# Two transformer blocks on one core: the rotary step's exchange of neighbouring partitions, by a shuffle on VectorE in place of a permutation matmul on TensorE

## What is computed

```python
def apply_rope(x, cos, sin):
    x1 = x[..., 0::2].astype(jnp.float32)
    x2 = x[..., 1::2].astype(jnp.float32)
    y1 = x1 * cos - x2 * sin
    y2 = x1 * sin + x2 * cos
    return jnp.stack([y1, y2], axis=-1).reshape(x.shape).astype(x.dtype)

# first_block, for each layer l:
q, k, v, up, ca, cb = project_inputs(h, w_in[l], q_norm_g[l], k_norm_g[l])   # q, k: rms_norm over 64 features of a head
q = apply_rope(q, cos, sin)
k = apply_rope(k, cos, sin)
k_all = jnp.concatenate([kc, k], axis=3)
attn = diff_attn_post(diff_attention(q, k_all, v_all, lam), subln_g[l], lambda_init)
conv_o = conformer_conv(ca, cb, conv_dw_w[l], ...)      # 31 taps
```

## Time and profile before

| | us |
|---|---|
| median of 3 runs (lowest, highest) | 1655.34 (1654.33, 1656.04) |
| span of the profiled execution | 1652.8 |
| PE busy in it | 1595.9 (97%) |
| DVE busy | 1120.9 (68%) |
| ACT busy | 921.6 (56%) |
| POOL busy | 132.4 (8%) |

### The profile page before, as it was taken

How to read it: one execution, slowest core, us unless ns; L and a number is a source line. 1 busy time by engine, 2 the same in 40 slices (tenths; PEclk the granted TensorE clock), 3 DMA queues, 4 the chain that set the end, 5 groups by cost and what they waited for, 6 DMA issues and landing times. The chain is left out here.

```text
span 1652.8 us, 31090 instructions
## 1 busy us (share of the span) xinstructions
PE 1595.9 (97%) x12890; PEld 1465.8 (89%) x12890; DVE 1120.9 (68%) x1763; ACT 921.6 (56%) x1467; POOL 132.4 (8%) x106
## 2 busy tenths in 40 slices
PE   5999989999999999989999999999999999999999
PEld 2987578999999999966899999878999998799999
DVE  2799667645566655897754556777887567788873
ACT  3444656645365444647554445766666467676662
POOL 0230000112001100300012100000011000001110
PEclk8999999999999999999999999999999999999999
DMA  9433666656546555435466553314555633235553
GB/s 386 161 147 142 255 230 232 228 223 233 194 167 222 200 187 200 154 128 217 172 216 201 187 198 130 117 56 144 194 200 187 216 118 118 78 132 203 206 190 120
DMA packets 45164, 301.09 MB, mean 182 GB/s; under 512 B 5232, under 2 KB 7504, under 8 KB 11744
## 3 DMA queue, kind: packets, MB, share of 16 engines
q1 hardware_dynamic: 44304, 297.44, 50.6%
q0 software_dynamic: 288, 0.92, 0.1%
q10 hardware_dynamic: 432, 0.75, 0.1%
HBM read 298.02 MB, written 1.06 MB: 181 GB/s over the span
## 5 line engine op out<-in xcount | busy, mean ns | idle before, releaser
L2018 DVE TENSOR_TENSOR wl<-raw,wh 128x1040 fp32r<-128x1040 f32 (+1 forms) x472 | 567.3, 1241 | 313.1 <-ACT wh L1771 220.6
L1771 ACT ACTIVATE wh<-raw 128x1040 fp32r<-128x1040 f32 (+1 forms) x472 | 465.5, 1030 | 182.7 <-PE bank L1560 95.2
L1555 PE MATMUL bank<-hx_hi,wh 128*128 128x256 f32 x1856 | 522.6, 282 | 6.0 <-ACT hx_hi L1771 3.8
L1560 PE MATMUL bank<-hx_lo,wh 128*128 128x256 f32 x1856 | 516.7, 278 | 0.0
L1558 PE MATMUL bank<-hx_hi,wl 128*128 128x256 f32 x1856 | 514.6, 277 | 0.2 <-DVE wl L2018 0.2
L1555 PEld LDWEIGHTS bank<-hx_hi,wh 128*128 128x128 f32 x1856 | 349.1, 188 | 12.8 <-issue 11.8
L1558 PEld LDWEIGHTS bank<-hx_hi,wl 128*128 128x128 f32 x1856 | 349.0, 188 | 4.3 <-issue 3.6
L1560 PEld LDWEIGHTS bank<-hx_lo,wh 128*128 128x128 f32 x1856 | 348.9, 188 | 1.2 <-DVE hx_lo L2011 0.4
L1558 PE MATMUL bank<-hid_hi,wl 128*128 128x256 f32 x912 | 252.2, 277 | 1.1 <-DVE wl L2018 1.1
L1555 PE MATMUL bank<-hid_hi,wh 128*128 128x256 f32 x912 | 252.4, 277 | 0.1
L1560 PE MATMUL bank<-hid_lo,wh 128*128 128x256 f32 x912 | 252.0, 276 | 0.0
(11 more groups left out here) (219 smaller groups left out, 1909.1 us busy)
## 6 DMA issues: line engine op xcount, KB each, us to landing
raw<-in_wts SPq DMA_DIRECT2D x208, 1032.0 KB, 4.9
raw<-in_wts SPq DMA_DIRECT2D x50, 1024.0 KB, 6.5
raw<-in_wts SPq DMA_DIRECT2D x20, 776.0 KB, 4.2
raw<-in_wts SPq DMA_DIRECT2D x4, 584.0 KB, 4.2
tmp<-tscr SPq DMA_DIRECT2D x16, 128.0 KB, 3.9
raw<-in_wts SPq DMA_DIRECT2D x2, 648.0 KB, 3.9
xTc<-in_ctxT SPq DMA_DIRECT2D x1, 1024.0 KB, 10.8
xTx<-in_xT SPq DMA_DIRECT2D x1, 1024.0 KB, 8.1
```

Of the source, the lines that this page charges most:

```text
L1555: pe.matmul(out, block(f, M.wh, w0 + k, ncols, c, m), x_hi, start=first and k == 0 and o == 0, stop=False, skip_group_check=True)
L1560: ins = pe.matmul(out, block(f, M.wh, w0 + k, ncols, c, m), x_lo, start=False, stop=last and k == nk - 1, skip_group_check=True)
L1771: return act.activation(out, in_, func, bias=bias, scale=scale)
L2018: tt(M.wl[k][:, cols], M.raw[r][:, cols], M.wh[k][:, cols].bitcast(F32), ALU.subtract).then_inc(*on.inc(lo))
```

## The change

In the rotary step of the first block the neighbour's value no longer comes from PE. DVE copies `xg` into `y` with the partitions of each pair exchanged (`stream_shuffle`, the pattern `PAIRS` applies to every group of 32 partitions), waits for that, and multiplies `y` with the sines in place. The signs that the permutation matrix held now lie in the table of sines. The matrix leaves the constants (`cst` 128x768 becomes 128x640; the memory behind it stays unused, so that all other addresses remain). Bank `r` and the event `t_r` go; DVE waits for ACT's `xg` (`t_xg`) instead.

```diff
+PAIRS = [i ^ 1 for i in range(32)]
...
-    j1 = np.zeros((P, P))
-    for i in range(64):
-        j1[2 * i + 1, 2 * i] = -1
-        j1[2 * i, 2 * i + 1] = 1
-    c["swap1"] = j1
...
-    sn = np.sin(ang.astype(np.float64))[:, dim].T
+    sn = np.sin(ang.astype(np.float64))[:, dim].T * np.where(np.arange(P) % 2, 1, -1)[:, None]
...
-        cst = sb("cst", [P, 6 * P])
+        cst = sb("cst", [P, 5 * P])
+        cur[0] += 4 * P
...
             s, t_s = banks.get(), ev("mm")
-            r, t_r = (None, None) if swap is None else (banks.get(), ev("mm"))
-            s_free, r_free = s.free, r and r.free
+            s_free = s.free
...
-                y, t_d = tmps.get(), [ev("rope") for _ in range(4)]
+                y, t_d = tmps.get(), [ev("rope") for _ in range(5)]
                 y_free = y.free
-                banks.give(r, t_d[0])
...
-            tmps.give(xg, t_d[0] if swap is None else t_d[2])
+            tmps.give(xg, t_d[0] if tables is None else t_d[3])
...
 # tensor_program
-    def hn2(s, s_free, r, r_free, sq, t_sq, xg, t_xg, blk, swap, np_, t_s, t_r, **_):
+    def hn2(s, s_free, sq, t_sq, blk, np_, t_s, **_):
         on.wait_ge(t_sq, s_free)
         mm(s.t[0:np_, :], blk, sq.t[0:np_, :], True, True).then_inc(*on.inc(t_s))
-        if swap is not None:
-            on.wait_ge(t_xg, r_free)
-            mm(r.t[0:np_, :], swap, xg.t[0:np_, :], True, True).then_inc(*on.inc(t_r))
...
 # vector_program, hn2
-        on.wait_ge(t_r, t_tab, y_free)
-        tt(v(y.t), v(r.t), wide(S), ALU.mult).then_inc(*on.inc(t_d[0]))
-        tt(v(xg.t), v(xg.t), wide(C), ALU.mult).then_inc(*on.inc(t_d[1]))
-        on.wait_ge(t_d[1])
-        tt(v(y.t), v(y.t), v(xg.t), ALU.add).then_inc(*on.inc(t_d[2]))
-        on.wait_ge(t_d[2], t_rs, out_free)
-        tt(out, v(y.t), v(rs.t), ALU.mult).then_inc(*on.inc(t_d[3]))
+        on.wait_ge(t_xg, t_tab, y_free)
+        dve.stream_shuffle(y.t[:, :], xg.t[:, :], PAIRS).then_inc(*on.inc(t_d[0]))
+        on.wait_ge(t_d[0])
+        tt(v(y.t), v(y.t), wide(S), ALU.mult).then_inc(*on.inc(t_d[1]))
+        tt(v(xg.t), v(xg.t), wide(C), ALU.mult).then_inc(*on.inc(t_d[2]))
+        on.wait_ge(t_d[2])
+        tt(v(y.t), v(y.t), v(xg.t), ALU.add).then_inc(*on.inc(t_d[3]))
+        on.wait_ge(t_d[3], t_rs, out_free)
+        tt(out, v(y.t), v(rs.t), ALU.mult).then_inc(*on.inc(t_d[4]))
```

More of the change, by code:

```diff
@@ L91, in shape_constants @@
     c["flip"] = np.eye(P)[::-1]
-    sq = np.concatenate([c[k] for k in ("ident", "ones", "bones", "swap1", "swap2", "flip")], axis=1)
+    sq = np.concatenate([c[k] for k in ("ident", "ones", "bones", "swap2", "flip")], axis=1)
     t = np.arange(T)
@@ L219, in __init__ @@
         b1_off = cur[0]
-        self.ident, self.ones, self.bones, self.swap1, self.swap2, self.flip = (
-            cst[:, P * i:P * i + P] for i in range(6))
+        self.ident, self.ones, self.bones, self.swap2, self.flip = (
+            cst[:, P * i:P * i + P] for i in range(5))
         self.V = lambda k: vec[:, VT[k][0]:VT[k][0] + VT[k][1]]
@@ L626, in plan_program, with heads_norm @@
     region_free = []
-    def heads_norm(b, tok, gain, nfeat, blk, swap, tables, out, out_free, np_=P):
+    def heads_norm(b, tok, gain, nfeat, blk, tables, out, out_free, np_=P):
         sq, xg = tmps.get(), tmps.get()
@@ L642, in rest @@
             banks.give(s, t_ln)
-            if swap is None:
+            if tables is None:
                 y, y_free, t_d = None, None, [ev("rope")]
             else:
-                y, t_d = tmps.get(), [ev("rope") for _ in range(4)]
+                y, t_d = tmps.get(), [ev("rope") for _ in range(5)]
                 y_free = y.free
-                banks.give(r, t_d[0])
-            step("hn2", s=s, s_free=s_free, r=r, r_free=r_free, sq=sq, t_sq=t_sq, xg=xg, t_xg=t_xg, rs=rs,
-                 rs_free=rs_free, y=y, y_free=y_free, blk=blk, swap=swap, tables=tables, nfeat=nfeat, np_=np_,
-                 out=out, out_free=out_free, t_s=t_s, t_r=t_r, t_ln=t_ln, t_rs=t_rs, t_d=t_d)
-            tmps.give(xg, t_d[0] if swap is None else t_d[2])
+            step("hn2", s=s, s_free=s_free, sq=sq, t_sq=t_sq, xg=xg, t_xg=t_xg, rs=rs,
+                 rs_free=rs_free, y=y, y_free=y_free, blk=blk, tables=tables, nfeat=nfeat, np_=np_,
+                 out=out, out_free=out_free, t_s=t_s, t_ln=t_ln, t_rs=t_rs, t_d=t_d)
+            tmps.give(xg, t_d[0] if tables is None else t_d[3])
             if y:
@@ L739, in project1 @@
             rest = heads_norm(b, tk, M.V(("qg" if part[0] == "q" else "kg", l)), 64, M.bones,
-                              M.swap1 if s == "x" else None, (M.cosx, M.sinx, t_b1), out, flat(ow))
+                              (M.cosx, M.sinx, t_b1) if s == "x" else None, out, flat(ow))
             def fin():
@@ L1214, in dil_piece @@
                 i = j % 2
-                rest = heads_norm(b, tk, M.V(("gdq" if j < 2 else "gdk", l)), 64, M.bones, None, None,
+                rest = heads_norm(b, tk, M.V(("gdq" if j < 2 else "gdk", l)), 64, M.bones, None,
                                   dst[:, 2 * i:2 * i + 2, :], rf)
@@ L2070, in modend, with hn2 @@
                     ALU.mult).then_inc(*on.inc(t_s[2 + s]))
-    def hn2(r, xg, t_xg, rs, y, y_free, tables, np_, out, out_free, t_r, t_rs, t_d, **_):
+    def hn2(xg, t_xg, rs, y, y_free, tables, np_, out, out_free, t_rs, t_d, **_):
         v = lambda x: x[0:np_, :].rearrange("p (a t) -> p a t", a=2)
-        if r is None:
+        if tables is None:
             on.wait_ge(t_xg, t_rs, out_free)
```

## The result

| | before | after |
|---|---|---|
| median of 5 runs (lowest, highest), us | 1655.27 (1653.64, 1656.04) | 1661.08 (1659.71, 1663.43) |
| span of the profiled execution, us | 1652.8 | 1659.2 |

The ratio is 1.0039, with a 95% interval of 1.0028 to 1.0050. The change makes the kernel slower, by 4.6 to 8.3 us, where I had +2.8 as likeliest and "no difference that can be told" as the likeliest outcome. The time lies inside my range, but the change is twice the one forecast. The profiled execution is 6.4 us longer, and its two traces can be laid side by side, since nearly every instruction has its counterpart.

The account below looks back on a forecast made before the run. DVE's queue, not PE, was taken to pace the changed stretches. First layer 0.57, second layer 2.4 and start -0.15 summed to +2.8 us, 1655.3 to 1658.2 us; range 1653.5 to 1661.5.

Parts of the forecast that it names:

- d = 0.80: DVE time in us added per shuffle at eight places: 0.72 for the shuffle, 0.08 for its pattern; bounds 0.49 and 1.2.
- Rival 1: The shuffle is dear on DVE, d 0.9 to 1.2, giving 1658.9 to 1660.9 us; chance 0.33.
- PE's start at the k1 gemm: First layer, about 138 us: the gemm inherits the matmul's wait and starts some 0.7 us later, not 2.66 us earlier.
- My three signs of being wrong: DVE idle for PE at 140 to 168 us; shuffle far from 0.8 us; PE's 1.31 us wait at 739.63 not growing.
- takes back 0.86 us with the fourth matmul: First layer, 156 us: PE regains 0.86 us, so is about where it was at 172.95, its sum over the taps.
- 4d - 2.63 = 0.57: First layer: four shuffles delay DVE by 3.2 us, less 2.63 us of slack at its end; loss 0.57 us.
- 3d = 2.4: Second layer: three of four shuffles delay the last taps, which PE awaits at 739.63 without slack; loss 2.4 us.
- The third shuffle: Second layer, q1: hidden, since DVE's 0.98 us wait for ACT at 727.61 takes in one d of 0.80.
- The wait at 739.63: Second layer: PE's wait for DVE's last taps was to grow from 1.31 to about 4 us or more.
- Start, -0.15: Load at the start: constants smaller by one 128x128 matrix, 64 KB, save 0.15 us, or zero if the load's end doesn't matter.
- another loss, of a few us: Remaining case: a loss in the tight web of attention units at 170 to 210 us; chance 0.05.

Follow-up runs that it names:

- the four superfluous matmuls: Changed kernel with q1's sum of squares (x, first layer) done five times instead of once, in PE's idle time ahead of the k1 gemm: 1.0017, 1658.51 us.
- the old constants: Changed kernel, all eight shuffles, but constants kept at 128x768: 1.0036 to the kernel before.
- the filler: Same run as the four superfluous matmuls: 512-column matmuls added to the changed kernel at q1 of x, first layer: 1.0017, 1658.51 us.
- the kernel with shuffles and late taps: Changed kernel with eight convolution taps moved from ahead of the first layer's first maxima to behind its first attention weights: 1.0024, 1659.94 us.
- the one with four late taps: Kernel before, permutation matmuls kept, with four taps moved behind the first layer's first attention weights: 0.9993, 1654.51 us.
- the small fillers: Changed kernel with four superfluous matmuls of 128 columns instead of 512, ahead of the first layer's k1 gemm: 1.0030, 1660.63 us.

## Why the prediction was wrong

**The shuffle's price: right.** d = 0.80 was forecast and 0.77 measured (0.74 us long, eight of them between 0.72 and 0.75). The pattern's load is 0.01 to 0.02 us and not 0.08. Rival 1, the dear shuffle, is out, though the outcome it stood for (slower) came. The estimate from the Trainium skill (VectorE: DVE Perf Modes, The perf-mode tier table (the rule you actually need)), 0.80 us long, was 0.06 too high, and the charge of its section The TRN2 errata for PSUM sources is not seen: 0.68 from PSUM, 0.69 from SBUF.

**PE's start at the k1 gemm: about right in time, wrong in what follows.** I forecast it some 0.7 us later than before; in the trace it is 0.2 later, or 1.1 when the start's -0.91 is taken out. I also named the reason, that the wait for the exponentials only passes from the matmul to the gemm. What I did not ask is what 5 us of idle time do to PE. My three signs of being wrong did not catch it: DVE shows no idle time for PE from 140 to 168 us. The step that failed is the sentence that PE "takes back 0.86 us with the fourth matmul (at 156 us), and is about where it was when it reaches the row at 172.95". It would be, at full clock. The gemm took 2.4 us longer, and behind it PE and no longer DVE is late at the end of the layer: in the earlier trace rows the sum over the taps starts at 172.95; after, it starts at 174.76, 2.5 us after the taps are done (170.99 + 1.27).

**First layer, 4d - 2.63 = 0.57: wrong, and in two ways.** With the clock kept up by the four superfluous matmuls, the layer ends 1.06 us later by its own start (the split at 99.71 comes at 98.50, the weights' use at 177.54 at 177.39). So DVE's part was 1.06 us; with the measured d the term gives 0.45. The slack was 2.06 us, DVE's own wait for PE's sum, and not 2.63: I added 0.57 us that stand behind the weights, but the convolution's chain through ACT (175.76, waiting 0.58 us) had no such reserve. The rest of 2.72 us, 1.7 us, is the clock in this pair of traces. It is not a fixed price: with the old constants and with shuffles in the first layer only, the clock falls too, the gemm takes 7.4 and 7.6 us instead of 8.4, and the product with v, at 202.88 us after, comes 1.7 and 1.9 us later than before by its own start, which leaves the clock 0.6 and 0.9 us. In the first of them part of the time at the lower clock passed while PE was idle.

**Second layer, 3d = 2.4: right.** 2.58 in the trace and +2.5 us in the run with the second layer alone. The third shuffle was hidden as forecast: the wait of 0.98 us ahead of q1's last multiplication is 0.19 after. The wait at 739.63 did grow, but only from 1.31 to 1.49 us, and not to 4: the gemm ahead of it ran at a clock of 0.50 (730 to 735 us, behind 4.08 us of idle time) and filled the gap. In six other traces with one shuffle at each place of this layer, as here, the wait was 1.64 us once and shrank five times, to 0.18 to 0.53 us, though the shuffles were there. So that row misleads as a test: it was one of my three signs of being wrong. The multiplication beside GpSimd's last work was slowed to 1.25 us in q0's step, in place of the add in the earlier trace rows.

**Start, -0.15: not seen**, and not to be seen, since the start differs by more than that from one execution to another.

**Not in the sum at all:** the clock of the first layer (1.7 us in the trace), the half microsecond in the output projection, where the clock is at 0.50 in both kernels but for longer after, and the late weights at 784 us (1.2 us). Of my cases the remaining one, with a chance of 0.05 for "another loss, of a few us", comes nearest, but I had placed it at 170 to 210 us and had no clock in mind. With the filler, whose trace has neither the first nor the last of these, the kernel measures +2.8 us (1.3 to 4.1), which is the sum that I had forecast. That it agrees to the tenth is luck, as the first layer's term was 0.6 us too small.

## What to carry to other kernels

When an edit takes work off an engine that then waits for another, write down how long its new idle time is, and look at the granted clock behind the idle times that the profile already has. At this gemm 1.5 to 1.8 us of it left the clock alone, and 3.6 us and more did not; elsewhere in the same traces two shorter waits close together were enough. Work taken off TensorE beside a queue of VectorE can then be worth nothing (1.0006 for eight matmuls left out), and work moved from the first to the second can be paid twice, in VectorE's queue and in TensorE's clock. A busy share of 97% says neither which engine paces a stretch nor what its matmuls would cost at full clock.

## What the runs showed of the hardware

- At the k1 gemm of the first layer the granted clock fell to 0.50 with idle times of PE of 3.60, 4.12, 4.81, 4.94, 5.06, 5.23 and 6.47 us, and stayed at 1.00 with 1.45, 1.48, 1.61 and 1.80 us. In the two kernels with 4.12 and 4.81 us the first matmul of the gemm still took the 0.36 us of full clock, and the fall came within it. Two short idle times in a row (0.88 us at 152.17, 1.50 us at 154.11) were followed by a fall too, in the kernel with shuffles and late taps. So were 1.31 and 1.89 us (at 739.63 and 742.62) in the kernel before, and 0.70 and 0.60 us (at 723.08 and 725.48) in the one with four late taps, so no single length of one wait divides the cases. The kernel before:

```profile
744.00:745.00 1.00, 1.00 (x3) 0.50 (x2) 0.90 (x5) 0.69 (x2) 0.00 (x0) 0.53 0.00 0
745.00:746.00 1.00, 1.00 (x4) 0.67 (x2) 0.96 (x2) 1.00 (x4) 0.00 (x0) 0.50 0.00 0
```

- Matmuls of 128x256 in f32 inside a gemm take 0.28 us at a granted clock of 1.00 and 0.41 us at 0.50; the gemm as a whole went from 6.0 to 8.4 us, with the lower clock for some 6 us of it, and took 7.2 to 8.5 us in the six other traces where the clock fell.
- A shuffle of 128x512 in f32 costs VectorE 0.72 to 0.75 us, its pattern load 0.01 to 0.02 us.
- Pieces of the instruction stream (0.02 MB each, 102 of them in the run) come over the DMA engines that also carry the weights. Where one came together with three weight transfers or behind their issue, the wait at 784 us stood in the trace (five traces), and two of the transfers landed in 7.5 us after, instead of 5.7 with the small fillers. The cause is inferred.
